# A hybrid conv and MoE layer on one core: twenty-three small columns moved in front of the weight buffers

## The chip, the core and the metric

The kernel runs on one NeuronCore of a Trainium2 chip. A core has TensorE (PE, matmuls), VectorE (DVE), ScalarE (ACT), GpSimd (POOL) and SyncE (SP), each with an instruction stream of its own; they meet only at semaphores. SBUF is the on-chip memory of 128 partitions, PSUM the accumulators. Sixteen DMA engines carry data between the chip's main memory (HBM) and SBUF. The metric is device time in microseconds of one execution, as a median over several runs; lower is better.

## The reference

One inference step of a one-layer trunk for 256 prompt rows and 8 streams of 16 rows, 384 rows of 1024 features in all, in float32:

```python
xn = rms_norm(x, norm1_g)
b_a, c_a, h_a, glu_a, glu_b, g_in = jnp.split(xn @ w_in, SPLITS, axis=-1)
conv_a, new_a = causal_depthwise_conv(c_a * h_a, buf_a, conv_a_w)              # 3 taps
y_a = (b_a * conv_a) @ w_out_a
conv_b, new_b = causal_depthwise_conv(glu_a * sigmoid(glu_b), buf_b, conv_b_w)  # 31 taps
y_b = silu(layer_norm(conv_b + conv_b_b, ln_b_g, ln_b_b)) @ w_out_b + b_out_b
x = x + (g_a * y_a + g_b * y_b) @ w_o
# MoE: the best of 4 groups, then the best 2 of its 8 experts, 32 experts in all
for e in range(N_EXPERTS):
    out = out + combine[:, e:e + 1] * ((silu(xn @ w_gate[e]) * (xn @ w_up[e])) @ w_down[e])
y = rms_norm(x + out, final_norm_g)
```

Every expert has three matrices of 2 MB (1024 x 512 and 512 x 1024, float32). All 32 are read, 201 MB in the end, beside 42 MB of the other weights.

## The kernel before

**First part, up to about 390 us.** The 40 MB of projection weights come in 40 units of 1 MB (4 x 128 rows by 512 columns), through three buffers `raw` (DMA issued by SP at L497). A unit's row in a partition is four separate pieces of 2 KB. ACT rounds each unit to its high part (`w_hi`, L720), POOL subtracts (`w_lo`, L601), and PE multiplies high and low parts with those of the activations (L1401), three matmuls for each product. DVE runs the 31-tap convolution beside it (L1052); its source starts one float (4 bytes) later with each tap. Then come the router and the tables that say which rows go to which expert.

**Second part, up to about 821 us.** Each expert's 6 MB come as six loads of 1 MB into buffers `piece`, 24 of them in four sets of six. SP issues them in a fixed order of sets (L547), each as soon as PE has used what stood in that buffer. The partition's part of such a load is one contiguous row of 8,192 bytes. PE works through items (32 rows of one expert): gate and up (L1570), the gather of the next item (L1521), adding back the last one (L1558) and down (L1599). There are 44 items for the 32 experts. The tail normalises the sum and writes it out.

**Where things lie.** Tensors are allocated one behind another in each partition. The first, `same`, starts at byte 1,152. Behind it stand `tmp`, `ident`, `iota` and `small`, then `halves`, one block of 24 x 8,192 bytes, then a tensor `few` of 24 columns. All of `raw`, `w_hi`, `w_lo`, `x_lo`, `in_hi`, `cvb`, `n_tok`, `merged`, `ua`, `ub`, `x_tok`, `stage`, `rw`, `vec` and all `piece` buffers are laid inside `halves` at fixed distances from its start, `halves_at`. Up to `small` the sizes add to 24,576 + 6,144 + 512 + 128 + 128 bytes, so `halves_at` is 1,152 + 31,488 = 32,640 = 255 x 128, and an assertion holds it at a multiple of 128. Since 8,192 is one as well, every `raw` and every `piece` row starts at a multiple of 128 bytes; it is 128 bytes past a multiple of 256.

`few` carries: `norm2_by_row` (8 columns, read by DVE at L1237 for each item), `mark` and `zero` (targets of tiny instructions that only advance a semaphore or load a table), `own_slot` and `slot_coef` (one column each, used for each item at L1259, L901, L1283, L1289, L1293 and L1297), and `second_sums` (3 columns, in the tail at L923 and L1319).

Of the kernel before, what the change touches and what calls it, by code (L numbers as in the profile page):

```python
# [33 lines left out]
P = 128  # L34


def trunk_program(nc, x_prompt, x_sample, cache_a, cache_b, norm1_g, w_in, gate_b, conv_a_w, w_out_a, conv_b_w,
# [6 lines left out]
    N = NP + NS * TS  # L44
    NT = N // P
    KB = D // P
# [6 lines left out]
    T = 32  # L53
# [97 lines left out]
    with ExitStack() as ctx:  # L151
        def sb(name, shape, dt=F32):
            return ctx.enter_context(nc.sbuf_tensor(name, shape, dt))

        def sem(name):
            return ctx.enter_context(nc.semaphore(name))
# [6 lines left out]
        tmp = sb("tmp", [P, HALF // P, N])  # L163
        ident = sb("ident", [P, P])
        iota = sb("iota", [P, T])
        small = sb("small", [P, 32])
        same_at = nc.sbuf_base - 4 * (2 * KB * N + 4 * N + P + T + 32)
        tmp_at = same_at + 2 * ACTS
        halves_at = nc.sbuf_base
        assert halves_at % 128 == 0  # L170
        halves = sb("halves", [P, HALVES * 2048])
        few = sb("few", [P, 24])
        norm2_by_row, mark, zero = few[:, 0:KB], few[:, 8:14], few[0:1, 14:18]
        own_slot, slot_coef, second_sums = few[:, 18:19], few[:, 19:20], few[:, 20:20 + NT]

        def at(name, shape, dt, offset):
            return nc.alloc_sbuf_tensor_at(name, shape, dt, offset=offset)
# [11 lines left out]
        def late(name, shape, dt=F32):  # L189

            offset = late_at[0]
            late_at[0] += -(-math.prod(shape[1:]) * (2 if dt == BF16 else 4) // 32) * 32
            assert late_at[0] <= halves_at + HALVES * UNIT
            return at(name, shape, dt, offset)
# [69 lines left out]
        lane = late("lane", [P, 1])  # L264
        rbias = late("rbias", [P, R])[:, :]
        down_rank = late("down_rank", [P, NE])[:, :]

        ua_k = ua[:, :].rearrange("p (k n) -> p k n", k=KB)
        ub_k = ub[:, :].rearrange("p (k n) -> p k n", k=KB)
# [52 lines left out]
        ssq_ready = sem("ssq_ready")  # L322
# [147 lines left out]
        def total(t, h):  # L470

            return bank[2 + 2 * t + h]
# [178 lines left out]
        def _(act):  # L651
# [263 lines left out]
            def last_square(n, h):  # L915

                i = LAST_ORDER[n]
                if n or h:
                    act.wait_ge(ssq_ready, 2 * NT + 2 * n + h)
                if h:  # L920
                    act.wait_ge(weighted, 2 * n + 1)
                sums = (small[:, 16:16 + NT], second_sums)[h]
                act.activation(squares[:, :], total(i, h)[:, :], ACT.Square, scale=1.0 / ROOT_D,  # L923
                               accum_out=sums[:, i:i + 1]).then_inc(ssq_ready, 1)

            def root(n):

# [11 lines left out]

            act.wait_ge(combined, items * NT + NT)  # L940
            last_square(0, 0)
            last_square(0, 1)
            act.wait_ge(combined, items * NT + (NT + 1))
            last_square(1, 0)
            last_square(1, 1)
            root(0)
# [11 lines left out]
        def _(dve):  # L958
# [8 lines left out]
            def rms_scale(n_ssq, n_root, src, mid, root, inv):  # L967
# [15 lines left out]
                                     accum_out=move_col[:, 0:1]).then_inc(order_consts, 1)  # L983
# [5 lines left out]
                                     accum_out=small[:, NT - 1:NT]).then_inc(ssq_ready, 1)  # L989
# [244 lines left out]
            def take_gathered(n):  # L1234
# [10 lines left out]
                                          accum_out=place))  # L1245
# [69 lines left out]
            def mean_square(n):  # L1315

                i = LAST_ORDER[n]
                dve.wait_ge(ssq_ready, 2 * NT + 2 * n + 2)
                dve.scalar_tensor_tensor(small[:, 20 + i:21 + i], small[:, 16 + i:17 + i], 1e-6, second_sums[:, i:i + 1],  # L1319
                                         ALU.add, ALU.add).then_inc(root_in, 1)  # L1320

            def inverse_root(n):
# [18 lines left out]
            weight(1, 1)  # L1341
            weight(1, 0)
            mean_square(0)
            mean_square(1)
            inverse_root(0)
            weight(2, 1)
            scale(0)
            inverse_root(1)
            weight(2, 0)
            mean_square(2)  # L1350
            scale(1)
            inverse_root(2)
# [301 lines left out]
```

## Time and profile before

| | |
|---|---|
| median of 3 runs | 847.16 us (846.04 to 847.32) |
| the profiled execution | 846.04 us, its span 844.3 us |
| PE / DVE / ACT / POOL busy | 92% / 51% / 38% / 31% of the span |
| mean DMA rate | 296 GB/s over the span, 422 GB/s from about 425 us on |

The span runs from the first to the last recorded instruction; 1.7 us of the execution lie outside it. In the timeline of forty slices each slice is 21.1 us. "DMA share" is the mean share of time in which the 16 DMA engines were carrying packets; a share of 1.01 means that packets follow one another with a slight overlap.

### The profile page before, as it was taken

The page shows a single profiled execution, that of the slowest core. Times are in us where ns is not written, and L with a number is a line of the kernel's source. Part 1 is how long each engine was busy: PE and PEld are TensorE (multiplying, and loading weights), DVE is VectorE, ACT ScalarE, POOL GpSimd, SP SyncE. Part 2 cuts the span into 40 slices and gives each one's busy share as a digit, 9 for nine tenths or more (in the row PEclk, how much of TensorE's full clock was granted, in tenths as well). Part 3 has the DMA queues.
Part 4 walks back from the last instruction along what each step waited for, and adds up shares of the span by engine and source line. Part 5 has one row for each costly group of instructions (what it writes and reads, how often), then busy time and mean ns, then how long its engine had stood idle before and what let it go on. Part 6 is the DMA issues. An engine that isn't in the chain of part 4 may idle for free.

```text
span 844.3 us, 21580 instructions
## 1 busy us (share of the span) xinstructions
PE 774.4 (92%) x8655; PEld 590.3 (70%) x8656; DVE 426.7 (51%) x1142; ACT 323.7 (38%) x559; POOL 258.5 (31%) x129
## 2 busy tenths in 40 slices
PE   3999999999999999999999989999898879979954
PEld 3999999999999999865555545555555545545532
DVE  4046978899994344153444433445434434434424
ACT  5333666555335833152322322322322223222224
POOL 3745699978677778300000000000000000000000
PEclk9999999999999999998999998999999999999997
DMA  7734343424444745974799999999999999999992
GB/s 250 231 101 150 101 125 125 151 98 144 146 169 150 297 150 220 336 298 151 310 423 422 422 422 422 422 422 422 422 422 422 422 422 422 422 422 422 422 422 120
DMA packets 53172, 249.99 MB, mean 296 GB/s; under 512 B 6599, under 2 KB 6599, under 8 KB 28561
## 3 DMA queue, kind: packets, MB, share of 16 engines
q1 hardware_dynamic: 49760, 246.95, 74.0%
q10 hardware_dynamic: 3377, 2.57, 1.2%
q8 instruction: 22, 0.36, 0.2%
q14 instruction: 13, 0.11, 0.0%
HBM read 246.76 MB, written 2.75 MB: 296 GB/s over the span
## 4 chain that ended last, share of the span: by engine, by line
PE 62%; DMA 18%; DVE 11%; SPq 3%; ACT 3%; issue 2%; POOL 1%; ACTq 0%; DVEq 0%
PE bank L1401 25%; DMA piece<-in_exp_w_up 17%; PE bank L1570 12%; DVE bank L1052 7%; PE bank L1599 7%; PE bank L1521 5%; PE bank L1558 5%; PE bank L1399 4%; SPq L547 3%; PE bank L1586 1%; DMA raw<-in_w_in 1%; PE bank L1528 1%; DVE sq L1114 1%; ACT w_hi L720 1%; PE bank L1462 1%
## 5 line engine op out<-in xcount | busy, mean ns | idle before, releaser
L601 POOL TENSOR_TENSOR w_lo<-raw,w_hi 128x2048 fp32r<-128x2048 f32 x40 | 185.0, 4627 | 75.3 <-ACT w_hi L720 75.2
L1570 PE MATMUL bank<-piece,xe 128*32 128x256 f32 x2816 | 169.2, 392 | 32.4 <-DMA piece<-in_exp_w_up 26.7
L1570 PEld LDWEIGHTS bank<-piece,xe 128*32 128x32 f32 x2816 | 97.3, 113 | 99.0 <-issue 48.3
L1401 PE MATMUL bank<-x_hi,w_hi 128*128 128x384 f32 x448 | 150.8, 337 | 1.6 <-POOL w_lo L601 1.3
L1401 PE MATMUL bank<-x_hi,w_lo 128*128 128x384 f32 x448 | 149.7, 334 | 0.0
L1401 PE MATMUL bank<-x_lo,w_hi 128*128 128x384 f32 x448 | 149.7, 334 | 0.0
L1052 DVE SCALAR_TENSOR_TENSOR bank<-ub,vec,bank 128x256 f32<-128x256 f32 (+1 forms) x416 | 137.3, 420 | 0.0
L720 ACT ACTIVATE w_hi<-raw 128x2048 fp32r<-128x2048 f32 x40 | 76.6, 1918 | 83.0 <-PE bank L1401 71.2
L1283 DVE SCALAR_TENSOR_TENSOR silu_and_hid<-bank,few,silu_and_hid 64x256 f32<-64x256 f32 x44 | 21.5, 490 | 170.8 <-ACT silu_and_hid L901 170.8
L1599 PE MATMUL bank<-piece,hidT 128*32 128x256 f32 x1408 | 94.2, 384 | 5.5
L1401 PEld LDWEIGHTS bank<-x_hi,w_hi 128*128 128x128 f32 x448 | 84.1, 188 | 2.9 <-POOL w_lo L601 1.5
L1401 PEld LDWEIGHTS bank<-x_lo,w_hi 128*128 128x128 f32 x448 | 84.1, 188 | 0.3
L1401 PEld LDWEIGHTS bank<-x_hi,w_lo 128*128 128x128 f32 x448 | 84.1, 188 | 0.0
L908 ACT ACTIVATE y_hi<-bank 128x256 fp32r<-128x256 f32 x44 | 16.9, 385 | 143.3 <-PE bank L1599 143.3
L1521 PE MATMUL bank<-x_rows,pick 128*32 128x256 f32 x1080 | 67.0, 379 | 0.4 <-DVE pick L1229 0.4
L901 ACT ACT_TABLE_LOAD x44 | 56.5, 1283 | 22.1 <-DVE at_slot L1259 22.1
L1599 PEld LDWEIGHTS bank<-piece,hidT 128*32 128x32 f32 x1408 | 40.2, 109 | 32.2 <-issue 13.3
L901 ACT ACTIVATE silu_and_hid<-bank,few 64x256 f32<-64x256 f32 x44 | 20.6, 469 | 100.2 <-PE bank L1570 100.2
L1558 PEld LDWEIGHTS bank<-y_hi,back_to 32*128 32x128 f32 x540 | 25.8, 181 | 46.1 <-issue 45.6
L1558 PE MATMUL bank<-y_hi,back_to 32*128 32x256 f32 x540 | 52.9, 381 | 1.6 <-DVE y_lo L1302 1.5
L1521 PEld LDWEIGHTS bank<-x_rows,pick 128*32 128x32 f32 x1080 | 37.4, 111 | 21.8 <-DVE pick L1229 0.6
L1237 DVE TENSOR_TENSOR xe<-bank,few 128x256 f32<-128x256 f32 x45 | 19.1, 425 | 61.4 <-PE bank L1528 61.4
(231 smaller groups left out, 984.0 us busy)
## 6 DMA issues: line engine op xcount, KB each, us to landing
piece<-in_exp_w_down SPq DMA_DIRECT2D x64, 1024.0 KB, 26.6
piece<-in_exp_w_gate SPq DMA_DIRECT2D x64, 1024.0 KB, 25.8
piece<-in_exp_w_up SPq DMA_DIRECT2D x64, 1024.0 KB, 26.9
raw<-in_w_in SPq DMA_DIRECT2D x28, 1024.0 KB, 5.2
raw<-in_w_out_a SPq DMA_DIRECT2D x4, 1024.0 KB, 5.0
raw<-in_w_out_b SPq DMA_DIRECT2D x4, 1024.0 KB, 5.0
raw<-in_w_o SPq DMA_DIRECT2D x4, 1024.0 KB, 5.0
out<-n_out SPq DMA_DIRECT2D x3, 512.0 KB, 3.3
```

The costliest lines, as they stand in the source:

```text
L547: sp.dma_start(piece[n][:, :], src[bass.ds(e, 1), h, :, :].rearrange("e p x -> p (e x)"))\
L601: pool.tensor_tensor(w_lo[u % NW][:, :, :], raw[u % NW][:, :, :], w_hi[u % NW][:, :, :].bitcast(F32), ALU.subtract).then_inc(lo_ready, 1)
L720: act.activation(w_hi[u % NW][:, :, :], raw[u % NW][:, :, :], ACT.Copy).then_inc(hi_ready, 1)
L901: act.activation(sig, GU[0:2 * T, :], ACT.Silu, scale=slot_coef[0:2 * T, 0:1]).then_inc(sig_ready, 1)
L1052: ins = dve.scalar_tensor_tensor(done[part] if tap == KB_TAPS - 1 else acc[part], src, w, done[part] if tap == first else acc[part], ALU.m ...
L1283: dve.scalar_tensor_tensor(hid, GU[2 * T:4 * T, :], slot_coef[2 * T:4 * T, 0:1], sig, ALU.mult, ALU.mult)\
L1399: ins = pe.matmul(b, xp[:, k, cols], wp[:, k % UK, :], start=start, stop=stop)
L1401: ins = pe.matmul(b, wp[:, k % UK, cols], xp[:, k, :], start=start, stop=stop)
L1521: last = pe.matmul(G[q * T:(q + 1) * T, :], pick[:, i, :], x_rows[:, i, q * QE:(q + 1) * QE], start=(i == 0), stop=(i == NT - 1))
L1558: last = pe.matmul(total(t, q // 2)[:, cols], back_to[rows, t * P:(t + 1) * P], y[rows, :], start=False, stop=last_item and y is y_lo and ...
L1570: last = pe.matmul(GU[q * T:(q + 1) * T, :], xe[:, k, :], wide(pairs[q // 2], k)[:, q % 2 * QE:(q % 2 + 1) * QE], start=(k == 0), stop=(k ...
L1599: last = pe.matmul(Y[q * T:(q + 1) * T, :], hidT[:, k, :], deep(pairs[2], k)[:, q * QE:(q + 1) * QE], start=(k == 0), stop=(k == HK - 1))
```

## The change

No instruction is added, taken away or moved to another place on its engine. Only addresses change. `few` goes; `small` grows from 32 to 48 columns and takes over `mark`, `zero`, `own_slot`, `slot_coef` and the second sums in columns that it did not use; `norm2_by_row` becomes a tensor of its own, in front of `halves`. So 24 columns (96 bytes) that stood behind `halves` now stand in front of it, and `halves_at` becomes 32,640 + 96 = 32,736 = 1,023 x 32. With it everything in `halves` moves by 96 bytes: each row of `raw` and `piece` now starts at an odd multiple of 32 bytes, 224 bytes past a multiple of 256. The assertion on 128 is removed. What lies in `same`, `tmp`, `ident` and `iota` keeps its address.

```diff
         iota = sb("iota", [P, T])
-        small = sb("small", [P, 32])
-        same_at = nc.sbuf_base - 4 * (2 * KB * N + 4 * N + P + T + 32)
+        small = sb("small", [P, 48])
+        norm2_by_row = sb("norm2_by_row", [P, KB])
+        same_at = nc.sbuf_base - 4 * (2 * KB * N + 4 * N + P + T + 48 + KB)
         tmp_at = same_at + 2 * ACTS
         halves_at = nc.sbuf_base
-        assert halves_at % 128 == 0
         halves = sb("halves", [P, HALVES * 2048])
-        few = sb("few", [P, 24])
-        norm2_by_row, mark, zero = few[:, 0:KB], few[:, 8:14], few[0:1, 14:18]
-        own_slot, slot_coef, second_sums = few[:, 18:19], few[:, 19:20], few[:, 20:20 + NT]
...
+        mark = small[:, 36:36 + 6]
+        zero = small[0:1, 31:35]
+        own_slot = small[:, 45:46]
+        slot_coef = small[:, 46:47]
...
-                sums = (small[:, 16:16 + NT], second_sums)[h]
+                at_col = (16, 42)[h] + i
                 act.activation(squares[:, :], total(i, h)[:, :], ACT.Square, scale=1.0 / ROOT_D,
-                               accum_out=sums[:, i:i + 1]).then_inc(ssq_ready, 1)
+                               accum_out=small[:, at_col:at_col + 1]).then_inc(ssq_ready, 1)
...
-                dve.scalar_tensor_tensor(small[:, 20 + i:21 + i], small[:, 16 + i:17 + i], 1e-6, second_sums[:, i:i + 1],
+                dve.scalar_tensor_tensor(small[:, 20 + i:21 + i], small[:, 16 + i:17 + i], 1e-6, small[:, 42 + i:43 + i],
```

## Rows read from the trace of the kernel before

**Rows 1.** The page: busy time by engine, and the timeline of 40 slices.

```profile
PE 774.4 (92%) x8655; PEld 590.3 (70%) x8656; DVE 426.7 (51%) x1142; ACT 323.7 (38%) x559; POOL 258.5 (31%) x129
...
PE   3999999999999999999999989999898879979954
...
DMA  7734343424444745974799999999999999999992
```

**Rows 2.** Stretches: us, PE PEld DVE ACT POOL busy, PEclk, DMA share, GB/s.

```profile
200.00:300.00 100.00, 98.48 (x569) 97.24 (x568) 67.55 (x145) 55.99 (x71) 71.20 (x29) 1.00 0.51 181
420.00:430.00 10.00, 9.88 (x172) 5.81 (x168) 4.16 (x11) 3.07 (x6) 0.00 (x0) 1.00 0.91 360
425.00:821.00 396.00, 359.08 (x5840) 211.56 (x5832) 165.17 (x436) 110.84 (x197) 0.00 (x0) 0.98 1.01 422
```

**Rows 3.** The chain that ended last, from 775 us: start, us, what.

```profile
793.71 27.52 DMA piece<-in_exp_w_up
821.23 0.14 issue
821.36 3.58 PE bank L1570 x32
...
839.16 0.77 ACTq L151
```

**Rows 4.** Waits from 420 to 822 us: total, times, longest.

```profile
PE bank L1570 <- DMA piece<-in_exp_w_up: 26.7, 12, 3.0
...
SPq L547 <- PE bank L1599: 44.1, 20, 5.5
SPq L547 <- PE bank L1570: 32.1, 22, 6.2
```

**Rows 5.** DMA from 440 to 800 us: packets and sizes, then queue: packets, MB, share.

```profile
DMA packets 20858, 151.89 MB, mean 422 GB/s; under 512 B 2319, under 2 KB 2319, under 8 KB 2319
...
q1 hardware_dynamic: 20857, 151.87, 101.3%
```

**Rows 6.** DMA from 340 to 349 us, the queue that ACT issues.

```profile
q10 hardware_dynamic: 2640, 0.17, 19.5%
```

**Rows 7.** Tile raw: instructions (ns min/median/max), ACT's idle before it, time to landing.

```profile
L720 ACT ACTIVATE w_hi<-raw x40: 1901/1916/2092, 12.6 to 338.4; 128x2048 fp32r<-128x2048 f32 x40
L601 POOL TENSOR_TENSOR w_lo<-raw,w_hi x40: 4537/4622/4926, 14.6 to 340.4; 128x2048 fp32r<-128x2048 f32 x40
...
  PE bank L1401: 71.2, 16
  DMA raw<-in_w_in: 8.4, 2
...
DMA to landing us min/median/max: 4.9/5.1/10.8
```

**Rows 8.** DVE's taps, 60 to 240 us, shapes apart: busy us, mean ns.

```profile
L1052 DVE SCALAR_TENSOR_TENSOR bank<-ub,vec,bank 128x256 f32<-128x256 f32 x206 | 100.3, 487 | 0.0
L1052 DVE SCALAR_TENSOR_TENSOR bank<-ub,vec,bank 128x128 f32<-128x128 f32 x207 | 73.2, 354 | 0.0
```

**Rows 9.** Line L1052 over the run: ns min/median/max.

```profile
L1052 DVE SCALAR_TENSOR_TENSOR bank<-ub,vec,bank x416: 345/421/497, 58.8 to 238.3; 128x256 f32<-128x256 f32 x70, 128x128 f32<-128x128 f32 x69
```

**Rows 10.** Tile few: the instructions of each item that read it.

```profile
L1237 DVE TENSOR_TENSOR xe<-bank,few x45: 414/425/427, 384.2 to 827.5; 128x256 f32<-128x256 f32 x45
L1259 DVE SCALAR_TENSOR_TENSOR at_slot<-x2T,few x45: 1017/1019/1020, 388.1 to 830.4; 128x768 f32<-128x768 f32 x45
```

## The prediction

> **What bounds the kernel now.** I read the timeline of forty slices first. PE is at nine tenths nearly everywhere; the DMA row is between 2 and 7 for the first half and then stands at 9 from slice 20 until the end [rows 1]. So there are two halves with different limits. Next, the stretches: from 200 to 300 us PE is busy 98.5 of 100 us while the DMA share is 0.51; from 425 to 821 us the DMA share is 1.01 at 422 GB/s and PE is busy 359 of 396 us [rows 2]. In the first part PE is the limit, in the second the DMA engines: they are never without a packet, whatever PE does. The chain that ended last says the same: the last load of an expert's weights is issued at 793.7 us and lands at 821.2 us, PE starts on it at 821.4 us, and the run ends some 18 to 23 us later [rows 3]. The waits are small on both sides, 26.7 us of PE on a load against 76 us of SP on PE [rows 4], but SP's waits cost nothing while the queue before it is full, and a share of 1.01 says that it is.
>
> The end of the second part is therefore "about 425 us, plus bytes over rate". Each engine moves rows of 8,192 bytes, one per partition and load. From 440 to 800 us there are 20,857 packets, 2,319 of them tiny; the other 18,538 are such rows (18,538 x 8,192 = 151.9 MB) [rows 5]. With 16 engines and 360 us, one row takes 16 x 360 / 18,538 = 0.3107 us of an engine. From 425 to 821.2 us that is 396.2 / 0.3107 = 1,275 rows on each engine, one behind the other. 32 bytes of such a row take 310.7 / 256 = 1.21 ns. A nanosecond more per row is 1.3 us at the end, and nothing beside it hides that.
>
> **The change, part by part.** (1) *The small columns themselves.* The same instructions read and write the same shapes at another address. DVE's item instructions on them take 425 and 1,019 ns, within 13 ns of one another over 45 executions [rows 10], and DVE is busy 165 of 396 us [rows 2]. Nothing is added: 0 us. Sharing `small` adds no wait, since the semaphores are untouched. In the tail, which is exposed, it is three additions on single columns: 0 us.
>
> (2) *Operands of the engines that now start 96 bytes later.* The trace has an experiment of its own for that: the convolution's source starts 4 bytes later with each tap, so it runs through all positions. Its two shapes take 487 and 354 ns in the mean [rows 8], and over all 416 executions the shortest is 345 and the longest 497 ns [rows 9]. Each shape thus stays within about 10 ns of its mean, with no place for a position that costs more. I take 0 for DVE and, by likeness, for ACT, POOL and PE. The other bound for PE: 1 ns more on each of the 1,344 matmuls of L1401 is 1.3 us in the first part, where PE is the limit. Both ends go into the range; I take 0, as the row for DVE is the nearest there is.
>
> (3) *Loads of the first part (40 MB in rows of 2 KB).* They land after 5.1 us, and ACT, which waits for them, was held up by loads only twice (8.4 us, at the start), but 16 times by PE (71.2 us, 4.5 us each time) [rows 7]. If each load took a quarter longer, 1.3 us, that would go into those 4.5 us. Cost 0; at the start, where two waits on loads are exposed, at most some 2 us.
>
> (4) *Loads of the second part.* Here is the whole question. Each of 1,275 rows per engine is written to an address that was a multiple of 128 and is now only a multiple of 32. If the write costs the same, nothing changes. If it costs more, it is paid in full. No row of the trace shows a long row at such an address. The nearest are the router's weights and biases: ACT's queue carries 2,640 packets of 0.17 MB from 340 to 349 us [rows 6]. By the code they go to addresses at all multiples of 16 (rows of 36 floats, cut at column 4). 19.5% of 16 x 9 us is 28.1 us, 10.6 ns per packet, for a mean of 64 bytes; two times 1.21 ns of that is the data. So 8.2 ns is all that is left for a packet's ordinary overhead and for whatever its start address costs. This bounds a cost that is paid once for each row: between 0 and 8.2 ns, 0 and 10.5 us. It doesn't bound one that is paid again and again inside a long row, since these packets are too short to have an inside.
>
> A page speaks on it. The Trainium skill, "DMA: Bandwidth & Descriptors", section "How a descriptor splits into AXI transactions", says that transfers are cut at multiples of 256 bytes and that one which starts past such a boundary pays for the bytes back to it, in steps of 32 bytes. It says so of reading; the sources are unchanged here. If writes did the same, a row would pay 4 steps before and 7 after. The short packets above agree with a small cost and cannot tell it from none. "SBUF — State Buffer", section "Door 1", has each port carry 32 bytes at a time, by which an address at a multiple of 32 costs nothing.
>
> I take 0 for (4), and so the forecast is **no change**: 847.0 us. The sum: the profiled execution is 846.04 us, 844.3 of span and 1.7 around it; plus 0 + 0 + 0 + 0; it lies 1.1 us under the median of 847.16, and what I predict is a median, so 847.0 with 845.4 to 848.7 for this case.
>
> **The rivals.**
>
> *A. A dearer edge of each row.* The first and last stretch of a row are cut differently: 128 bytes to the next multiple of 256 before, 32 bytes now. Such a cost is paid once per row. One step of 32 bytes: 1,275 x 1.21 ns = 1.5 us. Three steps (96 bytes, the shift itself): 4.6 us. The bound from the short packets: 10.5 us. For it: no cover at all in the second part, and rows not at any round address. Against it: before, rows are 128 bytes past a multiple of 256 already and the engines still move 422 GB/s with no gap. Value taken: 4.6 us, 851.6 us; from 848.5 to 857.5.
>
> *B. A cost inside the row, which ends slower by per cents.* If a row is written in chunks counted from its own start, each chunk at an odd multiple of 32 touches one wider line more than before. One step of 32 bytes more for each 512 bytes is 16 steps, 19.4 ns per row, 24.7 us: 871.7 us. One for each 256 bytes is 32 steps, 38.8 ns, 49.4 us: 896.4 us. More than that is possible. It decides as soon as the row of 310.7 ns becomes longer, since no slack stands before it; PE would then idle 60 to 90 us in the second part rather than 37. For it: the full exposure, and that nothing in the trace speaks against it; against it: only that 32 bytes looks like the unit in which these engines move data.
>
> *C. Faster.* The new distance between what PE reads in `same` and what the DMA writes in `halves`, or a shorter last chunk, could help. At 101% share a gain would have to come from the row itself; one step less is 1.5 us. 845.0 us or a little below.
>
> *D. The change does nothing at all to addresses.* It could be that the allocator rounds `halves` up to a round address. The built offsets say no (32,640 and 32,736), and the assertion on 128, which would fail, is taken out.
>
> **How the numbers follow.** No change 0.42; A 0.27; B 0.25, of which 0.11 up to some 874 us and 0.14 beyond; C 0.06. The last two decimals are judgement: the forecast rests on a guess of the write's unit, and the trace has no row that denies a slower one. A measurement of this kernel can tell about 0.2%, 1.7 us, from no change (the three runs spread over 1.3 us). C is the chance of faster, 0.06. Within 0.2% are the no-change case and the smallest of A, 0.42 + 0.03 = 0.45. Slower is the rest, 0.49: it is more than "same" only as a sum of cases that lie far apart, and none of them alone is likelier than no change, so the time stays at 847.0. The range leaves out B beyond 874 us (0.14) and what lies under 845.0 us (0.05): 845.0 to 874.0 us.
>
> **What would show it.** Right: from 440 to 800 us again 422 GB/s, 18,538 rows of 8 KB, the last load landing near 821 us, PE's waits on loads near 27 us, `raw` landing after 5.1 us, DVE's taps at 487 and 354 ns. A: 420 to 417 GB/s in that stretch, the last landing 2 to 10 us later, `raw` after 5.1 to 5.3 us. B: 397 GB/s (16 steps) or 375 GB/s (32 steps), the last landing 25 to 50 us later, PE busy under 0.85 of the second part, and `raw` after 5.4 to 5.7 us with the first part's end unchanged. What would make the prediction wrong beyond all this is a change of the first part's end, 390 us, with every instruction of L1401, L601 and L720 at its old duration, or one of these durations moved: then (2) was wrong, not (4).

## The result, and the profile after

| | before | after |
|---|---|---|
| median of 6 runs each | 846.27 us (845.88 to 847.32) | 850.87 us (848.34 to 852.11) |
| ratio to before, 95% | | 1.0051 (1.0037 to 1.0064) |
| the profiled execution | 846.04 us, span 844.3 | 847.72 us, span 845.2 |
| mean granted clock of its TensorE | | 0.981 |

The kernel is slower by 4.6 us. The profiled execution of after was the fastest of its kernel (the other spans go from 846.6 to 850.3 us), so its trace shows less of the loss than the medians do.

The first view is the page: the busy times, and the costliest groups of instructions, with the mean ns of one behind the busy time. First those of before, which were not shown ahead.

```profile
L1401 PE MATMUL bank<-x_hi,w_hi 128*128 128x384 f32 x448 | 150.8, 337 | 1.6 <-POOL w_lo L601 1.3
L1401 PE MATMUL bank<-x_hi,w_lo 128*128 128x384 f32 x448 | 149.7, 334 | 0.0
L1401 PE MATMUL bank<-x_lo,w_hi 128*128 128x384 f32 x448 | 149.7, 334 | 0.0
```

Then those of after.

```profile
PE 777.2 (92%) x8655; PEld 593.2 (70%) x8656; DVE 427.1 (51%) x1142; ACT 323.2 (38%) x559; POOL 258.5 (31%) x129
...
L1402 PE MATMUL bank<-x_hi,w_hi 128*128 128x384 f32 x448 | 152.6, 341 | 1.2 <-POOL w_lo L602 1.1
L1402 PE MATMUL bank<-x_hi,w_lo 128*128 128x384 f32 x448 | 151.0, 337 | 0.0
L1402 PE MATMUL bank<-x_lo,w_hi 128*128 128x384 f32 x448 | 150.4, 336 | 0.0
```

Every matmul of the projections takes 2 to 4 ns more. A matmul's time here spans two steps of PE, since it overlaps the next; the distance from one start to the next is about half of it. From the start times in the two traces I took the mean distances, by which operand moves and which is loaded, before and after: x_hi with w_hi 173.36 and 175.87 ns, x_lo with w_hi 173.20 and 174.20, x_hi with w_lo 173.65 and 174.55. That is 1.4 to 1.5 ns more in the mean. PE's total grew by 2.8 us, from the 774.4 us of [rows 1]. The line's first kind over the whole run (ns min/median/max, first and last start in us) shows where that arrives; first before, then after.

```profile
L1401 PE MATMUL bank<-x_hi,w_hi x448: 334/334/631, 19.2 to 295.5; 128*128 128x384 f32 x150
```

```profile
L1402 PE MATMUL bank<-x_hi,w_hi x448: 336/337/634, 18.9 to 296.9; 128*128 128x384 f32 x150
```

With the last output projection behind it (L1399, L1400 after), PE's first part, from the first start to the last, takes 343.2 us before (19.2 to 362.4) and 345.3 us after (18.9 to 364.1): **2.1 us** more.

Tile `raw` in the trace of after, as in [rows 7], says that neither ACT, POOL nor the loads do it: ACT and POOL take as long as before, they start their last unit 1.3 us later because PE frees the buffers later, and the loads land after the same 5.1 us.

```profile
L721 ACT ACTIVATE w_hi<-raw x40: 1897/1916/2100, 12.3 to 339.7; 128x2048 fp32r<-128x2048 f32 x40
L602 POOL TENSOR_TENSOR w_lo<-raw,w_hi x40: 4538/4622/4926, 14.3 to 341.7; 128x2048 fp32r<-128x2048 f32 x40
...
  PE bank L1402: 72.5, 16
  DMA raw<-in_w_in: 8.1, 2
...
DMA to landing us min/median/max: 4.9/5.1/10.4
```

Now the second part. The stretches of after (columns as in [rows 2]), then its DMA from 440 to 800 us, as in [rows 5].

```profile
200.00:300.00 100.00, 98.80 (x566) 97.55 (x565) 68.51 (x146) 55.11 (x71) 71.10 (x28) 1.00 0.52 181
425.00:821.00 396.00, 361.58 (x5853) 213.30 (x5852) 166.11 (x439) 110.72 (x198) 0.00 (x0) 0.98 1.01 421
```

```profile
DMA packets 20786, 151.34 MB, mean 420 GB/s; under 512 B 2314, under 2 KB 2314, under 8 KB 2314
...
q1 hardware_dynamic: 20785, 151.32, 101.3%
```

Rows of 8 KB are packets less the tiny ones: 18,472, where before there were 18,539 (the one packet of another queue counted in both). One row takes 16 x 360 us / 18,472 = 311.8 ns of an engine, 1.1 ns more than 310.7. Over 1,275 rows that is **1.4 us**. The engines are as full as before, so the row itself got dearer. The last pieces of the chain of after, as in [rows 3], put the landing of its last load at 823.8 us, 2.6 us later than before, though this load takes about as long (27.6 us). Two loads of `w_down` follow it in both kernels and are as much later (the last one lands at 826.2 and 828.8 us).

```profile
796.19 27.61 DMA piece<-in_exp_w_up
823.80 0.14 issue
823.93 1.93 PE bank L1571 x32
...
840.05 0.77 ACTq L151
```

PE's 32 matmuls behind it take 1.93 us here and 3.58 us in the trace of before [rows 3]. The stretches of just these matmuls, before and after, say why: the granted clock was 0.50, the lower of its levels (1.2 GHz), and 1.00.

```profile
821.50:824.90 3.40, 3.40 (x36) 2.17 (x35) 0.00 (x0) 0.00 (x0) 0.00 (x0) 0.50 1.00 414
```

```profile
824.00:826.00 2.00, 2.00 (x40) 1.47 (x44) 0.00 (x0) 0.07 (x1) 0.00 (x0) 1.00 1.04 430
```

In the pair n0, n1 below it is the other way round, 1.93 and 3.48 us, so it doesn't follow the change; it hid 1.65 us of the loss in this pair of traces. So the trace gives two terms, 2.1 and 1.4 us, in two parts of the run with nothing in common but the 96 bytes. Of their 3.5 us, 2.6 us arrive at the load in the chain.

### The profile page after: what moved, and what is told of

The parts are those of the page before. It is cut to its first block, busy times and chain, and to the rows that moved or that the text cites. A ratio compares the mean times of both kernels' runs of the same rounds, so it can differ in the third digit from the quotient of the medians.

```text
span 845.2 us, 21580 instructions
## 1 busy us (share of the span) xinstructions
PE 777.2 (92%) x8655; PEld 593.2 (70%) x8656; DVE 427.1 (51%) x1142; ACT 323.2 (38%) x559; POOL 258.5 (31%) x129
## 4 chain that ended last, share of the span: by engine, by line
PE 61%; DMA 21%; DVE 11%; ACT 3%; issue 2%; SPq 1%; POOL 1%; ACTq 0%; DVEq 0%
PE bank L1402 25%; DMA piece<-in_exp_w_up 20%; PE bank L1571 12%; DVE bank L1053 7%; PE bank L1600 7%; PE bank L1522 4%; PE bank L1559 4%; PE bank L1400 4%; PE bank L1587 1%; DVE sq L1115 1%; DMA raw<-in_w_in 1%; PE bank L1529 1%; SPq L548 1%; PE bank L1469 1%; PE bank L1463 1%
## 5 line engine op out<-in xcount | busy, mean ns | idle before, releaser
L1402 PE MATMUL bank<-x_hi,w_hi 128*128 128x384 f32 x448 | 152.6, 341 | 1.2 <-POOL w_lo L602 1.1
L1284 DVE SCALAR_TENSOR_TENSOR silu_and_hid<-bank,small,silu_and_hid 64x256 f32<-64x256 f32 x44 | 21.5, 489 | 170.3 <-ACT silu_and_hid L902 170.3
L902 ACT ACTIVATE silu_and_hid<-bank,small 64x256 f32<-64x256 f32 x44 | 20.6, 467 | 99.9 <-PE bank L1571 99.9
L1238 DVE TENSOR_TENSOR xe<-bank,norm_by_row 128x256 f32<-128x256 f32 x45 | 19.1, 424 | 61.6 <-PE bank L1529 61.6
```

What stands on the lines that cost most here:

```text
L902: act.activation(sig, GU[0:2 * T, :], ACT.Silu, scale=slot_coef[0:2 * T, 0:1]).then_inc(sig_ready, 1)
L1238: dve.tensor_tensor(xe[:, :, :].rearrange("p (q b) t -> p q b t", b=2), XT.rearrange("p (b q t) -> p q b t", b=2, q=TILES), norm2_by_row[: ...
L1284: dve.scalar_tensor_tensor(hid, GU[2 * T:4 * T, :], slot_coef[2 * T:4 * T, 0:1], sig, ALU.mult, ALU.mult)\
L1402: ins = pe.matmul(b, wp[:, k % UK, cols], xp[:, k, :], start=start, stop=stop)
```

## Experiments

### The parts moved one at a time

All kernels of this group share one frame, the computation being whole. The small columns are cut up so that they can lie anywhere: 16 that are needed early live inside `halves`, the others stand where two numbers say, in front of the halves or, in k3 and k5 in part or whole, behind them (not in the cut of the diff below). PE loads its five bounds of an item one by one, and six expert loads near 340 us are issued in another order. The frame costs 2.6 us, so its kernels are compared with one another. `HALVES_AT` places the `piece` buffers (with `ua`, `ub`, `x_tok`), `ARENA_AT` all of `raw`, `w_hi`, `w_lo`, `x_lo`, `in_hi`, `cvb` and `merged`; `same` with `x_hi` stays at 1,152.

```diff
-        HALVES_AT, ARENA_AT = 32640, 32640      # k0_as_before
+        HALVES_AT, ARENA_AT = 32736, 32736      # k1_as_after
+        HALVES_AT, ARENA_AT = 32736, 32640      # k2_pieces
+        HALVES_AT, ARENA_AT = 32640, 32544      # k3_arena
+        HALVES_AT, ARENA_AT = 32704, 32704      # k4_by64
+        HALVES_AT, ARENA_AT = 32512, 32512      # k5_by256
```

> The frame for the three beside it: halves and the first part's tensors at 32,640, as before. The small columns are split (16 of them used early live inside halves, 31 stand in front), PE loads its five item bounds one by one, and six expert loads near 340 us are issued in another order and a little later; the computation is whole. All theories expect the same: within 0.3% of the kernel before, 844 to 849 us, and matmuls of the projection line 173.4 ns apart as in the kernel before.

> The same frame with everything 96 bytes later, at 32,736, as in the changed kernel. All theories expect what the change gave, 1.003 to 1.007 of the frame at 32,640, some 4 us. If it came out equal, the loss would hang on where the small columns stand and not on the address of halves.

> Only the expert weights' buffers (with the convolution inputs, x_tok, stage and the router's weights) 96 bytes later, at 32,736; raw, w_hi, w_lo, x_lo, in_hi, cvb and merged stay at 32,640. Theory W (each 8 KB row that is written to an odd multiple of 32 bytes costs the DMA engine more): the whole loss, +4 us, and 311.8 ns per row as against 310.7. Theory M (PE's matmuls of the projections are slower with operands at an odd multiple of 32 bytes, the trace shows 174.8 ns from one to the next as against 173.4): matmuls at 173.4 again, and only the row term of the trace, +1 to +2 us, 0.1 to 0.2%.

> Only the first part's tensors (raw, w_hi, w_lo, x_lo, in_hi, cvb, merged) moved, 96 bytes down to 32,544, an odd multiple of 32; the expert buffers stay at 32,640. Theory W: the time of the frame, within 0.1%, since the loads of the first part are hidden. Theory M: matmuls of the projection line at 174.5 to 175 ns apart, the first part's end 1.5 to 3 us later and the time +1.5 to +3 us, 0.2 to 0.35%.

> The frame with everything in halves at 32,704, an odd multiple of 64. Theory 64 (the cost comes from addresses that are not a multiple of 64 bytes): the frame's own time, 849.0 us, within 0.1%, matmuls 173.4 ns apart, 310.7 ns per row. Theory 128 (a multiple of 128 is wanted): the time of the frame at 32,736, 853.7 us, with matmuls at 174.8 ns.

> The frame with everything in halves at 32,512, a multiple of 256. If a multiple of 128 already gives all there is, 849.0 us, within 0.1%, and 310.7 ns per row. If rows that start 128 bytes past a multiple of 256 pay for it, a row takes 305.8 ns (four steps of 1.21 ns less) and the time falls by some 6 us to 843 us.

Measured, with the ratio to the kernel before, the mean distance of two projection matmuls and the time of one 8 KB row between 440 and 800 us:

| | median us | ratio (95%) | to k0 | matmul ns | row ns |
|---|---|---|---|---|---|
| k0_as_before | 848.99 | 1.0025 (1.0016 to 1.0034) | | 173.4 | 310.8 |
| k1_as_after | 853.71 | 1.0088 (1.0074 to 1.0102) | +4.7 | 174.9 | 311.8 |
| k2_pieces | 850.08 | 1.0040 (1.0028 to 1.0052) | +1.1 | 173.4 | 311.8 |
| k3_arena | 853.53 | 1.0085 (1.0072 to 1.0098) | +4.5 | 175.6 | 310.7 |
| k4_by64 | 850.88 | 1.0050 (1.0035 to 1.0065) | +1.9 | 174.3 | 310.8 |
| k5_by256 | 852.61 | 1.0068 (1.0053 to 1.0084) | +3.6 | 175.6 | 306.8 |

The pair k0, k1 repeats the change: +4.7 us. The two terms come apart. k2 has the dearer row alone and costs 1.1 us, which the medians hardly tell from nothing (their intervals meet) and the row's time does; k3 has the unmoved row and the dearer matmul, by another distance (96 bytes back), and costs 4.5 us. The queue's rows from 440 to 800 us, first k2, then k3:

```profile
DMA packets 20785, 151.36 MB, mean 420 GB/s; under 512 B 2311, under 2 KB 2311, under 8 KB 2311
```

```profile
DMA packets 20859, 151.91 MB, mean 422 GB/s; under 512 B 2318, under 2 KB 2318, under 8 KB 2318
```

k5 says what counts is not how round an address is: its blocks in `halves` all start at multiples of 256, its row is the cheapest of all, and its matmuls are dear. These are its groups of the projection's line from 60 to 330 us (busy us, mean ns).

```profile
L1407 PE MATMUL bank<-x_hi,w_hi 128*128 128x384 f32 x374 | 128.8, 344 | 0.1
L1407 PE MATMUL bank<-x_hi,w_lo 128*128 128x384 f32 x375 | 126.6, 338 | 0.0
L1407 PE MATMUL bank<-x_lo,w_hi 128*128 128x384 f32 x374 | 124.3, 332 | 0.0
```

Times the line's 1,728 matmuls that I counted in a trace, the excess makes 2.6 us in k1, 3.9 in k3, 1.6 in k4 and 3.7 in k5. The first part itself grew by 2.2 us in the trace of k1 and 3.1 us in that of k5, so it doesn't pass on the whole sum.

Not all of k3's 4.5 us need be this excess. In its trace, and in that of k4, the line starts at about half its pace: 14 and 10 distances of 320 ns and a longer first one, which make 2.3 and 1.7 us, though the granted clock of the stretch reads 1.00. Without them the first part grew by 2.6 us in k3 and 1.5 us in k4. One of these matmuls of k3:

```profile
19.64 0.52 PE L1407 MATMUL bank<-x_lo,w_hi 128*128 128x384 f32 x1
```

The three kernels of matmuls alone, further below, start in the same way (15, 15 and 8 distances of 320 ns), and their first set is the one with all operands alike, so a dear layout isn't needed for it. What brings it about, and how many executions of k3 and k4 it met, stays open.

Three of these kernels missed what was expected of them. k3 lies over its 1.5 to 3 us, perhaps by that start; k4 has 174.3 ns, where one theory wanted 173.4 and the other 174.8; and k5, expected at 849 or 843 us, came to 852.61 us, since the expectation left its matmuls out of account.

### Moving `same` along

If the matmul's price lies in where its operands stand to one another, it must go when `same` moves too. k6 is k1 with 96 bytes in front of `same`; every operand of PE then stands 224 past a multiple of 256. k7 puts 128 bytes there, so `same` is at 1,280, and the halves at 32,512, all multiples of 256; `iota` goes behind the halves. k8 is k7 with the expert loads in the kernel's own order.

```diff
+        pad = sb("pad", [P, 24])                # k6_together; 32 columns in k7_all256
-        HALVES_AT, ARENA_AT = 32736, 32736
+        HALVES_AT, ARENA_AT = 32512, 32512      # k7_all256
```

> The frame with everything 96 bytes later, halves at 32,736 and with it same, tmp, ident and iota (same at 1,248), so all matmul operands start 224 bytes past a multiple of 256. Theory R (the matmuls lose time where the two activations, x_hi in same and x_lo in halves, and the weights stand at different positions within 256 bytes, since the frames at 32,736, 32,544, 32,704 and 32,512 had means of 174.9, 175.6, 174.3 and 175.6 ns and only equal positions 173.4): 173.4 ns, and of the loss only the rows' part, 1.4 us, 850.4 us. Theory P (a position at an odd multiple of 32 is slow in itself): 174.9 ns and 853.7 us, as the frame at 32,736.

> The frame with same at 1,280 and halves at 32,512, both multiples of 256; iota behind halves, the small columns in front of same. Theory R with the rows' price of the loads alone (306.6 ns at a multiple of 256): matmuls at 173.4 ns, rows at 306.8 ns, 1,275 x 4 ns = 5 us less DMA time; PE's own work then becomes the limit of the second part and takes back a part: 844 to 847 us as against 849.0. Theory P: the same.

> The layout of the kernel with all at multiples of 256, but with the expert loads issued in the order and at the waits of the kernel before (in the frame they came a little later, which cost 2.6 us). Expected by both: 2 to 3 us under the frame with that layout, 842 to 845 us, faster than the kernel before by 0.2 to 0.5%.

k6: 850.68 us, 1.0055 (1.0040 to 1.0069), +1.7 us on k0 and 3.0 us under k1. Its matmuls are back at 173.4 ns and its first part at 343.1 us, while its row stays at 311.8 ns. The same rows as of k5, now of k6:

```profile
L1408 PE MATMUL bank<-x_hi,w_hi 128*128 128x384 f32 x374 | 125.9, 337 | 0.2 <-DVE ua L1078 0.2
L1408 PE MATMUL bank<-x_hi,w_lo 128*128 128x384 f32 x375 | 125.3, 334 | 0.0
L1408 PE MATMUL bank<-x_lo,w_hi 128*128 128x384 f32 x375 | 125.3, 334 | 0.0
```

k7 and k8 (849.31 and 849.17 us, 1.0032 and 1.0033) have both the cheap matmul and a row of 306.7 ns, and yet gain nothing on k0, where 844 to 847 and 842 to 845 us were expected. The end of k7's chain tells why: it is PE alone, item after item. No load of an expert stands in the whole chain.

```profile
826.10 3.45 PE bank L1577 x64
829.55 1.29 PE bank L1528 x24
832.60 1.07 PE bank L1606 x16
```

The order of the expert loads, which k8 has as the kernel before has it, is not what the frame costs. What is left are the five loads of bounds, and the next group shows them: n3 differs from k8 only in loading the bounds at once, and takes 5.3 us less. A gain of the queue can't be read in a frame in which PE is the limit, so the last group goes without them.

### One-line pairs

Here PE keeps its single load of the bounds, and one line of it is written so that the limits of its registers are asserted and not taken over. n0 is otherwise the kernel before (the line costs 1.6 us), n1 the kernel after. n2 and n3 have the layouts of k6 and k7, the frame's small columns with them, with the kernel's own order of loads.

```diff
-                at_item = [pe.snap(x, min_val=0 if c == 0 else 1, max_val=MAX_ITEMS) for c, x in enumerate(bounds)]
+                at_item = [nc.s_assert_within(pe.snap(x, donate=True), 0 if c == 0 else 1, MAX_ITEMS) for c, x in enumerate(bounds)]
```

> The kernel before with one line changed: PE keeps its single load of the five item bounds and states their limits on the loaded registers. The baseline for the three beside it; 846 to 848 us, PE waiting some 25 us on loads in the second part as in the kernel before (in the frame, where PE loaded the bounds one by one, it hardly waited at all, so PE was level with the loads there).

> The changed kernel with the same one line. By the two terms found (moving operands at unlike positions, 2.0 us of the first part; rows, 1,275 x 1.1 ns = 1.4 us): +3.4 us, ratio 1.004. If there is a third cause, the measured +4.6 us stays unexplained by 1 us or more here too.

> The changed address of halves (32,736) with same, tmp, ident and iota 96 bytes later as well, expert loads in the kernel's own order, the small columns in front. By the two terms: only the rows remain, +1.4 us, ratio 1.0015 to 1.002. If the address itself cost more in the second part: +3 us or more.

> Everything at multiples of 256 (same 1,280, halves 32,512). Rows 306.7 ns rather than 310.7, first part unchanged. If the loads set the second part's end, up to 5 us faster, 842 us; if PE is close behind them, as in the frame, where nothing was gained, within 1.5 us of the baseline.

| | median us | ratio to before (95%) | to n0 | first part us | row ns |
|---|---|---|---|---|---|
| n0_before | 847.81 | 1.0019 (1.0006 to 1.0032) | | 343.1 | 310.8 |
| n1_after | 852.36 | 1.0072 (1.0052 to 1.0092) | +4.5 | 345.3 | 311.8 |
| n2_together | 849.30 | 1.0042 (1.0027 to 1.0057) | +1.5 | 343.1 | 311.8 |
| n3_all256 | 843.91 | 0.9970 (0.9958 to 0.9982) | -3.9 | 343.2 | 306.7 |

Of the loss of 4.5 us, 1.5 us stay when `same` moves along (the row, 1.4 by its price) and 3.1 us go (the matmuls, 2.2 by the first part). The medians are no sharper than that: their intervals reach 1.0 to 1.7 us to either side. n1 had been expected at +3.4 us, and by its expectation 1 us or more over that would stay unexplained; this is taken up at the end of the part on the prediction. n3 beats both kernels of this case by 2.3 and 7.0 us. Its queue from 440 to 800 us, its second part, and the last load in its chain:

```profile
DMA packets 21131, 153.87 MB, mean 427 GB/s; under 512 B 2350, under 2 KB 2350, under 8 KB 2350
...
q1 hardware_dynamic: 21130, 153.86, 101.1%
```

```profile
425.00:821.00 396.00, 365.56 (x5887) 214.85 (x5890) 166.12 (x439) 110.90 (x198) 0.00 (x0) 0.97 1.01 427
```

```profile
790.71 27.02 DMA piece<-in_exp_w_up
817.87 3.37 PE bank L1579 x32
```

In n0 that load is issued at 796.67 us. 1,275 rows at 4.1 ns less are 5.2 us; the last load is issued 6.0 us earlier, and the median keeps 3.9 us of it.

### Loads alone

m_dma has only loads of weights to SBUF, no computation; so it leaves the whole reference out. Rows of 8,192 bytes, then of 2,048, in nine and five stretches that differ in the start address.

> Loads alone, no engine computes (outputs are filled with copies of inputs; the whole computation is left out). 24 loads of 1 MB in rows of 8,192 bytes at each start address (bytes past a multiple of 256): 128, 224, 0, 32, 64, 96, 160, 192, 128; then 12 loads in rows of 2,048 bytes at 128, 224, 0, 32, 128. Theory W (an address at an odd multiple of 32 makes the write itself dearer): 311.8 ns per row of an engine at 224, 32, 96, 160 and 310.7 at the others. Theory C (the 1.1 ns come from meeting the engines' accesses): the same 310 ns at all addresses.

Its DMA rows for 56 us within the stretches that start at 224, 0, 32 and 96 past a multiple of 256, in this order:

```profile
DMA packets 3240, 23.61 MB, mean 422 GB/s; under 512 B 358, under 2 KB 358, under 8 KB 358
```

```profile
DMA packets 3287, 23.92 MB, mean 427 GB/s; under 512 B 367, under 2 KB 367, under 8 KB 367
```

```profile
DMA packets 3240, 23.59 MB, mean 421 GB/s; under 512 B 360, under 2 KB 360, under 8 KB 360
```

```profile
DMA packets 3247, 23.69 MB, mean 423 GB/s; under 512 B 355, under 2 KB 355, under 8 KB 355
```

Within each stretch (16 engines x the mean distance from one row's start to the next, without the first and last 7% of the rows), by the start past a multiple of 256:

| start | 0 | 32 | 64 | 96 | 128 | 160 | 192 | 224 |
|---|---|---|---|---|---|---|---|---|
| ns per 8,192 bytes | 306.8 | 311.4 | 310.3 | 310.1 | 310.1 | 310.1 | 310.3 | 311.4 |
| ns per 2,048 bytes | 80.2 | 84.8 | | | 84.6 | | | 84.6 |

There are three prices: the row that ends and starts on a multiple of 256; one that doesn't, 3.3 to 3.5 ns more; and one that has an edge of 32 bytes, in front (224) or behind (32), another 1.1 to 1.3 ns. The change goes from the second to the third. The first step is paid by the row and not by the byte, since each row of 2 KB pays it too (4.4 to 4.6 ns). The second shows in rows of 8 KB alone; rows of 2 KB cost the same at 128 and at 224, which agrees with the first part's loads landing as before. Theory W had wanted the dearer row at 96 and 160 too, and they are as cheap as 128.

The Trainium skill ("DMA: Bandwidth & Descriptors", section "How a descriptor splits into AXI transactions") has, for reading, a start past a boundary of 256 bytes pay for the bytes back to it in steps of 32. Were it so of these writes, then by an estimate with one step at the 1.21 ns of the prediction a start at 96 would cost 3.6 ns and one at 224 8.5 ns more than 0. The runs agree that the multiple of 256 is the cheapest; they don't show the steps, since all from 64 to 192 cost the same and 32 costs as much as 224.

### Matmuls alone

Three kernels hold only the projection's matmuls, in sets of 96 at chosen addresses, on operands filled with a constant; all the rest of the computation is left out. m_pe has weights at one place and both moving operands at another. m_pe2 takes the two moving operands apart. m_pe3 has all operands in one tensor, five patterns, and seven distances each.

```diff
-        COMBOS = [(0, 0), (96, 0), (0, 96), (96, 96), (32, 0), (0, 32), (32, 32), (64, 0), (0, 64), (64, 64), (0, 0)]
+        COMBOS = [(0, 0, 0), (0, 0, 0)] + [(d, 0, 0) for d in D] + [(0, d, d) for d in D] + [(0, 0, d) for d in D] \
+            + [(d, 0, d) for d in D] + [(d, d, d) for d in D] + [(0, 0, 0)]
```

> The projection's matmuls alone on constants (all else is left out; outputs are filled with copies of inputs), 96 for each pair of start addresses of the stationary and the moving operand (bytes past a multiple of 128): 0/0, 96/0, 0/96, 96/96, 32/0, 0/32, 32/32, 64/0, 0/64, 64/64, 0/0. Theory P (PE itself reads an operand at an odd multiple of 32 more slowly): 173.4 ns apart at 0/0 and 64, 174.5 to 176 where the operand concerned is at 32 or 96. Theory C (it is contention with the other engines or DMA, not PE's own read): 173.4 ns in all of them.

> Matmuls alone again (all else is left out), 96 for each set of positions of weights / x_hi / x_lo, in bytes past 128 of a multiple of 256: 0/0/0 twice, 96/0/96 (as the changed kernel), 160/0/160, 64/0/64, 128/0/128, 96/96/96, 160/160/160, 96/0/0, 0/0/96, 0/0/0. Theory R within PE alone: 173.3 ns at 0/0/0, 96/96/96 and 160/160/160, and 174.9, 175.6, 174.3, 175.6 for the four mixed sets. Theory C (it takes the other engines' accesses): 173.3 ns throughout but for small deviations that don't follow the kernel's.

> Only the projection's matmuls (weights 128x128, moving operand 128x384, float32 in PE's replicated form, three per product as on the projection's line); everything else is left out, so the output isn't the reference's. 38 sets of 96 matmuls, all operands in one tensor. A set is told by how far its weights, x_hi and x_lo stand past 128 of 256 bytes: two sets 0/0/0, then d/0/0, 0/d/d, 0/0/d, d/0/d and d/d/d, each with d = 32, 64 ... 224, then 0/0/0. Theory 1, only the two moving operands' places to one another count: d/0/0, 0/d/d and d/d/d stay at 173.3 ns per matmul for every d; 0/0/d and d/0/d cost 1 to 3.4 ns at d = 96, 128, 160. Against it speaks one set of the first matmul kernel, weights 0 and both moving operands at 96, at 176.7. Theory 2, what counts is where the operand in motion stands to the weights that are loaded beside it: 0/d/d costs as much as 0/0/d, d/d/d costs nothing, and d/0/0 should cost something at some d; it did not at 96. Theory 3, the place of a moving operand by itself: 0/d/d costs most and d/d/d the same. It fell for 96 and 160, and should fall for the other five.

The first set of each kernel holds the slow start and is left out. m_pe: every set at 173.3 to 173.6 ns per matmul but weights 0 and x 96, at 176.7. m_pe2, in weights / x_hi / x_lo: 0/0/0 173.3 and, as its last set, 173.6; 96/0/96 174.7, 160/0/160 176.6, 64/0/64 173.3, 128/0/128 175.5, 96/96/96 and 160/160/160 173.6, 96/0/0 173.4, 0/0/96 176.7. After m_pe2 I held that the two moving operands' places to one another decide. m_pe3 shows that this is not all. Its distances from start to start in ns:

| d | 32 | 64 | 96 | 128 | 160 | 192 | 224 |
|---|---|---|---|---|---|---|---|
| d/0/0 | 173.3 | 174.7 | 176.6 | 176.0 | 176.7 | 173.3 | 176.6 |
| 0/d/d | 173.3 | 173.5 | 176.6 | 176.0 | 173.4 | 174.7 | 173.5 |
| 0/0/d | 175.5 | 173.9 | 176.6 | 175.6 | 175.5 | 175.5 | 174.5 |
| d/0/d (the kernel's) | 174.5 | 173.3 | 174.8 | 175.6 | 175.6 | 174.1 | 174.1 |
| d/d/d | 173.6 | 173.6 | 173.6 | 173.6 | 173.6 | 173.6 | 173.6 |

The rows of the matmul line for the sets 0/0/0, 0/96/96, 96/0/96 and 96/96/96 (ns min/median/max of one, first and last start of 95):

```profile
L44 PE MATMUL bank<-free x95: 333/335/337, 32.1 to 48.4; 128*128 128x384 f32 x95
```

```profile
L44 PE MATMUL bank<-free x95: 336/338/343, 199.8 to 216.4; 128*128 128x384 f32 x95
```

```profile
L44 PE MATMUL bank<-free x95: 332/337/342, 435.0 to 451.4; 128*128 128x384 f32 x95
```

```profile
L44 PE MATMUL bank<-free x95: 333/335/347, 552.2 to 568.5; 128*128 128x384 f32 x95
```

Only what moves everything together is free at all seven distances (the last set, 0/0/0 again, has 173.6 ns too), so the price isn't in an address by itself but in where the operands stand to one another. The place of the weights counts: with both moving operands left alike, 0/96/96 costs as much as 0/0/96. The two moving operands' places to one another count as well: 0/32/32 and 0/160/160 are free, while 0/0/32 and 0/0/160, with the weights and x_lo in the same places, cost 2.1 to 2.2 ns more. So theory 2 is borne out at 96 and 128 and not at all distances; neither pair alone sets the price. And it is the kernel's price: the set 96/0/96 has 175.8, 174.2 and 174.5 ns for the three kinds of matmul; the kernel after has 175.87, 174.20 and 174.55. The set 128/0/128 repeats k5 (181.6, 170.2 and 175.0 ns, in k5 181.4, 170.2 and 175.1). DMA, DVE and ACT do nothing beside these matmuls. One case isn't repeated: 64/0/64 costs nothing alone, and k4, whose operands stand so, has 174.3 ns. What stays open is the rule for a given distance: 96/0/0 cost nothing in m_pe2 and 3.3 ns in m_pe3, where the buffers stand other multiples of 256 apart, so the distance past a multiple of 256 isn't all of it.

## Why the prediction was wrong

It said no change, 847.0 us; measured were 850.87 us, slower, inside the range of 845.0 to 874.0. Its base lay 0.7 us too high, since it went by the median of three runs (846.27 us is that of six), so what it missed is 4.6 us. Point by point:

(1) *The small columns, 0 us.* Right: the item instructions of L1237 and L1259 take in after what they took before (424 ns at L1238), and k6 and n2, whose columns stand elsewhere again, show no term of their own.

(2) *Operands of the engines, taken 0.* **This step failed**, for PE, and it is the larger term: 2.1 us in the trace. For DVE no cost shows: its taps take 480 and 348 ns after the change, for 487 and 354 [rows 8]. Those 6 to 7 ns aren't a gain of the layout either, since the pair n0, n1, with the same two layouts, has 483 and 484 ns for the larger shape.

```profile
L1053 DVE SCALAR_TENSOR_TENSOR bank<-ub,vec,bank 128x256 f32<-128x256 f32 x206 | 99.0, 480 | 0.0
L1053 DVE SCALAR_TENSOR_TENSOR bank<-ub,vec,bank 128x128 f32<-128x128 f32 x207 | 72.0, 348 | 0.0
```

The error was "by likeness" from DVE to PE. The taps change the place of one operand of an instruction. PE computes and loads weights at once (98.48 and 97.24 of 100 us [rows 2]), and the change moved the weights and x_lo away from x_hi, which stayed in `same`. No row for DVE could deny a cost of that. The other bound written down, "1 ns more on each of the 1,344 matmuls of L1401", was the right quantity with both factors too small: 1.4 to 1.5 ns, on 1,728 matmuls. (L1401 also has 384 matmuls of the convolutions' output projections.) That makes 2.5 us by the same arithmetic; the traces of three pairs show 2.1 to 2.2 us, and the medians of n1 against n2 3.1 us. Little hides it: the first part is PE's, and the steady row of expert loads begins only as PE gives the first part's buffers back.

(3) *Loads of the first part, 0 us.* Right, with landing after 5.1 us in both, and m_dma shows rows of 2 KB at the same 84.6 ns at the start before and the one after.

(4) *Loads of the second part, taken 0; rival A 4.6 us.* The row did get dearer: rival A's mechanism, an edge that is paid once per row with no cover. Of its three sizes the smallest holds, "One step of 32 bytes: 1,275 x 1.21 ns = 1.5 us", where 1.1 ns and 1.4 us were measured (k2 +1.1, n2 +1.5, k6 +1.7 us); that it is one step is in part luck, since m_dma shows no steps between 64 and 192. The short packets of [rows 6] gave 0 to 8.2 ns and could not choose; I chose by which unit the engines seem to use. The Trainium skill ("SBUF — State Buffer", section "Door 1") has a port carry 32 bytes at a time, and the prediction worked out from it that a start at a multiple of 32 costs nothing; k2 differs, with 1.1 ns more for just that.

Rival A's total came close (851.6 against 850.87 us), for half the wrong reason: its 4.6 us were to be all in the rows, with the first part unchanged. Its mark was also seen, 420 GB/s, but "the last landing 2 to 10 us later" (2.6 us) is more than half the first part's. The prediction had named the mark that tells the two apart: a change of the first part's end, or of a duration of L1401, and "then (2) was wrong, not (4)". That mark was seen; both were wrong. Rival B is out (420, not 397 GB/s), C is out for this address, but it was the right idea for another: n3's cheaper row is 4.1 ns. D is out.

By the traces the two terms sum to 1.4 + 2.1 = 3.5 us, for 4.6 measured, whose interval goes from 3.1 to 5.4 us. So about 1 us is not accounted for, and it may be noise. It is the same with the matmuls' term, 3.0 us in the medians of k1 and k6 and 2.1 us in the spans of their profiled executions. In the pair of n0 and n1 the rest can be placed: the span is 4.6 us longer, the first part 2.2 us, the load in the chain lands 3.0 us later, and the other 1.6 us are PE's first 32 matmuls behind it, which ran at the lower clock in n1. That the layout does this isn't shown: each of the two layouts has it in one trace of two (before and n1, but not n0 and after).

## What to carry to other kernels

Before allocations are shifted in a kernel whose PE or queue has no slack, write down the address past a multiple of 256 of each loaded row and of each matmul operand, before and after. Rows that start and end on multiples of 256 were the cheapest to load, and moving all blocks that PE reads together was the one move that cost nothing at every distance: the layout that does both gained 0.3% here, the one that does neither lost 0.5%. A likeness from one engine's rows is no bound for another engine that reads in another way.

## What was not expected of the hardware

- A matmul of 384 columns with a weight load beside it took 173.3 ns, and up to 176.7 ns, by nothing but its operands' addresses; moved together, all seven distances cost the same. Single kinds went from 169.3 to 181.6 ns, in sets whose means were 175.5 and 175.6.
- A DMA row of 8,192 bytes took 306.8 ns at a multiple of 256, 310.1 to 310.3 ns at 64 to 192 past one, and 311.4 ns at 32 and 224. A row of 2,048 bytes took 80.2 ns at a multiple of 256 and 84.6 to 84.8 ns elsewhere.
- A cheaper row was worth nothing where PE had become the limit (k7, 306.7 ns, no gain on k0), and 3.9 us where it had not (n3).
